# A hybrid decoder layer (HGRN2, S5, two SwiGLU FFNs): interleaved first weight blocks, and a last pair of tiles taken one tile at a time

## What is computed

```
h = concat([meta, x])                                            # 272 x 2048
h = h + 0.5 * swiglu(rms_norm(h, norm_ffn1), gate1, up1, down1)  # width 5632
h = h + mixer(rms_norm(h, norm_mix), ...)                        # HGRN2 + S5 branches, gates, w_out
h = h + 0.5 * swiglu(rms_norm(h, norm_ffn2), gate2, up2, down2)
out = rms_norm(h, norm_final)[16:]                               # 256 x 2048
```

## Time and profile before

| | us |
|---|---|
| median of 3 runs | 2337.34 (2336.91 to 2338.72) |
| the profiled execution | 2339.8 |
| its span, first to last instruction | 2338.1 |
| PE busy | 2308.5 (99%) |
| DVE, ACT, POOL busy | 1522.8, 1025.3, 179.8 |
| DMA, mean over the span | 175 GB/s |

### The profile page before, as it was taken

The page is one execution under the profiler, slowest core; times in us unless marked ns, Lnnn a source line. Parts: engine busy times, 40 slices in busy tenths (PEclk is TensorE's granted clock), DMA queues, the critical chain, the costliest instruction groups (busy, mean ns, idle before and its releaser), DMA issues.

```text
span 2338.1 us, 47313 instructions
## 1 busy us (share of the span) xinstructions
PE 2308.5 (99%) x17952; PEld 2203.8 (94%) x17952; DVE 1522.8 (65%) x2114; ACT 1025.3 (44%) x1251; POOL 179.8 (8%) x250
## 2 busy tenths in 40 slices
PE   8999999999999999999999999999999999999997
PEld 8999999999999999999999999998888888888886
DVE  6555544467554578888877766557776655666655
ACT  5334343445543443334555544445444433444443
POOL 0000010289200000001000000000000000000000
PEclk9999999999999999999999999999999999999999
DMA  7555555555555555554555545655666655656553
GB/s 220 176 174 172 173 175 178 173 172 170 180 174 175 171 166 169 162 170 145 161 158 165 152 143 175 200 186 177 192 181 184 193 187 186 183 183 195 187 187 119
DMA packets 416923, 408.67 MB, mean 175 GB/s; under 512 B 19408, under 2 KB 416720, under 8 KB 416848
## 3 DMA queue, kind: packets, MB, share of 16 engines
q1 hardware_dynamic: 411856, 407.03, 56.4%
q10 hardware_dynamic: 4992, 0.60, 0.2%
HBM read 405.48 MB, written 2.10 MB: 174 GB/s over the span
## 4 chain that ended last, share of the span: by engine, by line
PE 95%; DVE 3%; ACT 1%; issue 1%; DMA 0%; ACTq 0%; DVEq 0%; SPq 0%
PE ps L360 31%; PE ps L358 20%; PE ps L355 20%; PE ps L359 20%; DVE w_lo L899 1%; PE ps L528 0%; ACT w_hi L597 0%; PE ps L472 0%; DMA raw<-gate 0%; PE ps L521 0%; DVE scr L923 0%; DVE ks L1165 0%; ACT xs L619 0%; DVE qs L1166 0%; DVE h L1357 0%
## 5 line engine op out<-in xcount | busy, mean ns | idle before, releaser
L899 DVE TENSOR_TENSOR w_lo<-raw,w_hi 128x1024 fp32r<-128x1024 f32 x765 | 948.5, 1245 | 618.7 <-ACT w_hi L597 612.4
L360 PE MATMUL ps<-xs,w_lo 128*128 128x256 f32 (+2 forms) x4416 | 1258.3, 285 | 0.0
L597 ACT ACTIVATE w_hi<-raw 128x1024 fp32r<-128x1024 f32 x765 | 804.8, 1058 | 967.4 <-PE ps L360 959.9
L358 PE MATMUL ps<-xs,w_hi 128*128 128x272 f32 (+2 forms) x3008 | 864.5, 287 | 6.5 <-DVE w_lo L899 3.6
L359 PE MATMUL ps<-xs,w_hi 128*128 128x272 f32 (+2 forms) x3008 | 861.8, 287 | 0.0
L360 PEld LDWEIGHTS ps<-xs,w_lo 128*128 128x128 f32 x4416 | 833.9, 189 | 0.0
L358 PEld LDWEIGHTS ps<-xs,w_hi 128*128 128x128 f32 x3008 | 567.8, 189 | 11.7 <-issue 8.3
L359 PEld LDWEIGHTS ps<-xs,w_hi 128*128 128x128 f32 x3008 | 570.8, 190 | 0.0
L355 PE MATMUL ps<-xs,w_hi 128*128 128x512 f32 x1408 | 493.3, 395 | 0.3 <-DVE w_lo L899 0.3
L360 PE MATMUL ps<-hs,w_lo 128*128 (+2 forms) x1408 | 402.7, 286 | 0.0
L355 PEld LDWEIGHTS ps<-xs,w_hi 128*128 128x128 f32 x1408 | 264.5, 188 | 61.4 <-issue 0.6
(11 more groups left out here) (250 smaller groups left out, 1587.8 us busy)
## 6 DMA issues: line engine op xcount, KB each, us to landing
raw<-gate SPq DMA_DIRECT2D x176, 512.0 KB, 4.5
raw<-up SPq DMA_DIRECT2D x176, 512.0 KB, 3.8
raw<-down SPq DMA_DIRECT2D x176, 512.0 KB, 3.4
raw<-w_in SPq DMA_DIRECT2D x168, 512.0 KB, 3.5
raw<-w_out SPq DMA_DIRECT2D x32, 512.0 KB, 4.5
raw<-w_proj SPq DMA_DIRECT2D x24, 512.0 KB, 4.5
raw<-glu_a SPq DMA_DIRECT2D x8, 512.0 KB, 3.4
raw<-glu_b SPq DMA_DIRECT2D x8, 512.0 KB, 3.5
```

The costliest lines, as they stand in the source:

```text
L358: pe.matmul(out, hi, xh, start=start and k == 0, stop=False)
L360: last = pe.matmul(out, lo, xh, start=False, stop=stop and k == KT - 1)
L597: act.activation(w_hi[:, slot, :, :], raw[:, slot, :, :], ACT.Copy).then_inc(hi_ready, 1)
L899: tt(w_lo[:, slot, :, :], raw[:, slot, :, :], w_hi[:, slot, :, :].bitcast(f32), SUB).then_inc(lo_ready, 1)
```

## The change

At the start, gate and up units alternate: for each group `g` of four input tiles the gate unit (u = 2g) and the up unit (u = 2g + 1). The first group and its gate unit are loaded, split and multiplied in pieces of one or two tiles, and the next three units are split in halves. Meta tokens and `x` come as one array, so a row of a tile is 272 floats in one piece. The small parameters are loaded by SyncE in the second gate block. The norm stands ahead of unit 6. The warm-up has 9 matmuls of `ones` by `ones`.

At the end, the last pair of tiles is not wide and is taken tile by tile, with squares of its own; the two accumulators of squares are folded to one; the square root's table is loaded a pair earlier; VectorE makes all products, the first two tiles singly.

```diff
+STORES = ((0, 1), (1, 2)) + tuple((k, k + 2) for k in range(2, DT, 2))
-POOL_PAIRS = (3, 7)
@@ SyncE
             def load(j, w, group, col, u):
-                sp.wait_ge(lo_ready, u + 1)
+                if not isinstance(u, int) or u >= RING:
+                    sp.wait_ge(lo_ready, u + 1)
...
+            def load_x(k0, k1, landed):
+                sp.dma_start(h[:, k0:k1, :], hT.rearrange("(k p) t -> p k t", p=P)[:, k0:k1, :]).then_inc(landed, 16)
+            def load_first(w_gate, w_up):
+                for c, (k0, k1) in enumerate(((0, 1), (1, 2), (2, 4))):
+                    load_x(k0, k1, x_first[c] if c < 2 else x_in[0])
+                    sp.dma_start(raw[:, 0, k0:k1, :], w_gate.rearrange("(k p) n -> p k n", p=P)[:, k0:k1, 0:NC])\
+                        .then_inc(w_first[c] if c < 2 else raw_ready[0], 16)
+                for g in range(4):
+                    if g:
+                        load_x(4 * g, 4 * g + 4, x_in[g])
+                        load(2 * g % RING, w_gate, g, 0, 2 * g)
+                    load((2 * g + 1) % RING, w_up, g, 0, 2 * g + 1)
...
-                        column_block(w_gate, 0, 0, load_x)
-                        column_block(w_up, 0, 1)
-                    with sp.Fori(peeled, blocks) as b:
+                        load_first(w_gate, w_up)
+                        column_block(w_gate, NC, 2, load_small)
+                        column_block(w_up, NC, 3)
+                    with sp.Fori(2 * peeled, blocks) as b:
...
+            for c, (k0, k1) in enumerate(STORES):
+                sp.wait_ge(y_final, c + 1)
+                sp.dma_start(out[:, k0:k1, :], h[:, k0:k1, META:T]).then_inc(stored[c % 4], 16)
@@ TensorE
+                    if by_tile and c == 0 and k == KT - 1:
+                        last.then_inc(tile_done, 1)
...
-                        unit(j, (g + q) * 4 + j, 2 * j, n, rhs, start, stop, wide=wide)
+                        unit(j, (g + q) * 4 + j, 2 * j, n, rhs, start, stop,
+                             wide=wide and not (final and j == 3), by_tile=final and stop and j == 3)
...
+                if index == 3:
+                    total = ps[:, NORM_BANK[index], 0:T - c0]
+                    pe.wait_ge(tile_sq, 1)
+                    pe.matmul(total, ones[:, :], scr[:, 2, c0:T], start=True, stop=False)
+                    pe.wait_ge(folded, 1)
+                    pe.matmul(total, ones[:, :], scr[:, 4, c0:T], start=False, stop=False)
+                    pe.wait_ge(sq_ready, 8 * index + 8)
+                    pe.matmul(total, ones[:, :], scr[:, 3, c0:T], start=False, stop=True).then_inc(sq_used, 1)
+                    return
...
+                    def first_blocks():
+                        pe.wait_ge(gated, 1)
+                        pe.wait_ge(hidden, 1)
+                        for u in range(2 * RING):
+                            g, s = u // 2, u % 2
+                            if u == 6:
+                                norm(0, 0)
+                            unit(u % RING, u, 2 * s, T, rows(xs, 4 * g, 0, T), g == 0, g == 3, 4 * g)
...
-            pe.wait_ge(consts, 2)
-            keep_warm(14, 0)
+            pe.wait_ge(ones_ready, 1)
+            keep_warm(9, 0)
+            pe.wait_ge(consts, 1)
@@ ScalarE
+            def last_square(c):
+                if c:
+                    act.wait_ge(pair_out, 4 * PASSES_BEFORE[3])
+                else:
+                    act.wait_ge(summed, 6 * 3 + 5)
+                    act.wait_ge(tile_out, 1)
+                ins = act.activation(scr[:, 2 + c, META:T], h[:, DT - 2 + c, META:T], ACT.Square)
+                ins.then_inc(sq_ready if c else tile_sq, 1)
...
-                            if k == 7:
+                            if k == (6 if f else 7):
                                 load_sqrt()
+                            if f and k == 7:
+                                last_square(1)
+                                return
                             square(1 + 2 * f, c0, k)
+                            if f and k == 6:
+                                last_square(0)
...
+            first_split(1)
+            next_x(1)
+            first_split(2)
+            first_split(3)
+            next_x(2)
+            square(0, 0, 0)
+            square(0, 0, 1)
+            split(0, 1)
+            next_x(3)
+            square(0, 0, 2)
+            split(0, 2)
@@ VectorE, the last pass
+                        def residual_tile(c):
+                            row = h[:, DT - 2 + c, c0:T]
+                            if c == 0:
+                                dve.wait_ge(tile_done, 1)
+                            stt(row, ps[:, 6 + c, 0:T - c0], 0.5, row, MUL, ADD).then_inc(pair_out if c else tile_out, 1)
...
                         def add(j, p=p):
+                            if f and p and j == 3:
+                                residual_tile(0)
                             if 4 * p + j >= 2:
                                 add_squares(1 + 2 * f, c0, 4 * p + j - 1)
+                            if f and p and j == 3:
+                                dve.wait_ge(summed, 6 * 3 + 6)
+                                tt(scr[:, 4, c0:T], scr[:, 4, c0:T], scr[:, 5, c0:T], ADD).then_inc(folded, 1)
...
+            for k0, k1 in STORES:
+                dve.wait_ge(gained, k0 // 2 + 1)
+                y = h[:, k0:k1, META:T]
+                tt(y, y, scr[:, 5:6, META:T].broadcast_to([P, k1 - k0, SEQ]), MUL).then_inc(y_final, 1)
```

More of the change, by code:

```diff
@@ L340, in _, with unit @@
             pe.sem_inc(cx_done, 1)
-            def unit(j, u, banks, n, rhs, start, stop, need=None, wide=False):
-                pe.wait_ge(lo_ready, u + RING + 1)
+            def unit(j, u, banks, n, rhs, start, stop, need=None, wide=False, by_tile=False):
+                first = isinstance(u, int) and u < RING
+                if not first:
+                    pe.wait_ge(lo_ready, u + RING + 1)
                 by_column = [(c, k) for c in range(2) for k in range(KT)]
@@ L365, in keep_warm @@
                 for _ in range(n):
-                    pe.matmul(ps[:, bank, 0:P], ones[:, :], ident[:, :], start=True, stop=True)
+                    pe.matmul(ps[:, bank, 0:P], ones[:, :], ones[:, :], start=True, stop=True)
             def halves_of(x):
@@ L649, in block @@
                     def block(b, mean=False):
-                        for j in range(1 if mean and not f else 0, 4):
-                            split(b * 2 + q, j)
+                        start = mean and not f
+                        if not start:
+                            for j in range(4):
+                                split(b * 2 + q, j)
                         if mean:
                             root(2 * f, c0)
-                        split(b * 2 + q + 1, 0)
+                        split(b * 2 + q + 1, 2 if start else 0)
                         act.wait_ge(gated, b + done + 2)
                         act.activation(scr[:, 2:4, c0:T], scr[:, 0:2, c0:T], ACT.Sigmoid).then_inc(sig_ready, 1)
-                        for j in range(1, 4):
+                        for j in range(3 if start else 1, 4):
                             split(b * 2 + q + 1, j)
@@ new lines, in first_split, with next_x @@
+            def first_split(u):
+                act.wait_ge(raw_ready[u], 16)
+                for half in (slice(0, KT // 2), slice(KT // 2, KT)):
+                    act.activation(w_hi[:, u, half, :], raw[:, u, half, :], ACT.Copy)\
+                        .then_inc(hi_ready if half.start else first_hi, 1)
+            def next_x(g):
+                act.wait_ge(x_in[g], 16)
+                for k in range(4 * g, 4 * g + 4):
+                    upper(0, 0, k)
+            first_split(1)
+            next_x(1)
@@ L745, in _ @@
+            split(1, 0)
+            split(1, 1)
             ffn(0, 0, 0, parameters)
```

187 lines of the change are left out of this document (107 added, 80 removed).

## The result

| | us |
|---|---|
| median after, 7 runs | 2329.56 (2329.07 to 2331.26) |
| median before, beside them, 7 runs | 2337.60 (2336.91 to 2338.72) |
| ratio | 0.9967 [0.9957, 0.9976] |
| the profiled execution after, and its span | 2329.07, 2327.4 |

The change wins 8.0 us, or 7.8 against the median shown ahead. The prediction was 2325.9 with a range up to 2329.3: faster, as forecast, but 3.7 us short of the forecast and 0.3 outside its range.

A forecast was written before the change was run, and what follows sets the result against it. TensorE, busy throughout the middle, bounds the kernel, so only start and end can win: 8.2 + 1.2 + 2.2 - 0.15 = 11.4 us off the 2337.34 median gives 2325.9 us, range 2322.3 to 2329.3.

The forecast's parts named there:

- First piece: Kernel start: small first loads are in SBUF by about 4 us, so TensorE begins near 5.5 instead of 10.83.
- The stream: Start's loads: 5.37 MB up to the last x group, at 0.366 MB/us after 4 us, give its use at 17.8.
- behind it: From last x group to unit 8: splits, squares, norm and units 5 to 7 end at 34.5, 8.2 us won.
- Small loads move ... I take nothing: Seven small loads on SyncE's queue ahead of units 8 to 11: no cost; about 1 us once if cover failed.
- The end: Behind the last matmul: the root starts 1.2 us sooner; products and stores take 8.1 instead of 10.3, 2.2 us won.
- price of the five units: Five units no longer wide make 8 more matmuls each: cost between nothing and 0.5 us, taken as 0.15.
- The median of the runs is 2.5 lower: Conversion from the profiled execution, 2339.8, to the runs' median: a constant 2.5 us lower, so the gain applies in full.
- The first, the handing over slower than its parts: Start: costlier small copies, stream nearer 315 GB/s, a clock fall before the norm; start wins 5 to 6; chance 0.10.
- The second, the clock in the middle moving: Middle, low clock behind the 1351 us hole: the spell vanishes (2322.7) or a second comes (2329.1); chance 0.12.
- The third, the lower clock up to unit 8: Start: broken work keeps the lower clock until unit 8, which begins at 53; 2344 us, slower; chance 0.03.
- The fourth, only the first piece early: Start: last x is late anyway and only the first piece early; start wins 3, 2331 us; chance 0.05.
- What would show it: Signs in the changed profile: times for first matmul, last x, norm, unit 8, root and products, and no 0.50 clock between 10 and 40.

The follow-up runs named there:

- e4: The changed kernel with the first x group and first gate unit as one whole load each: median 2328.75 us, ratio 0.9960 to before.
- e1: The changed start with the end of before: median 2332.70 us, 5.5 us under before, ratio 0.9977.
- e5: The changed kernel repeated unaltered: median 2329.86 us, 8.6 us under before, ratio 0.9964.
- e13: The changed kernel run a third time, unaltered: median 2329.65 us, 8.9 us under before, ratio 0.9960.
- e11: Repeat of the changed kernel with first x group and first gate unit as whole loads: median 2329.23 us, 8.1 us under before, ratio 0.9961.
- e10: Repeat of the changed kernel with first x group and gate unit in two pieces of two tiles: median 2329.35 us, ratio 0.9962 to before.
- e8: Before, with only the seven small loads moved from ScalarE's to SyncE's queue and the three additions behind them: median 2334.99 us, 3.4 us under before.
- e3: Before, with VectorE making all last products and SyncE storing in nine pieces: median 2336.37 us, 1.9 us under before, ratio 0.9993.
- e2: The start of before with the changed end: median 2334.90 us, 3.3 us under before, ratio 0.9987.
- e9: The changed kernel with first x group and gate unit in pieces of one and three tiles: median 2328.83 us, 8.5 us under before, ratio 0.9963.
- e6: The changed kernel with the first gate unit's three pieces issued from ScalarE's queue: median 2329.66 us, 8.8 us under before, ratio 0.9963.
- e7: The changed kernel with first x group and gate unit in two pieces of two tiles, not three: median 2328.38 us, ratio 0.9958 to before.
- e12: Whole loads of first x group and gate unit in the changed kernel, with 16 warm-up matmuls instead of 9: median 2328.47 us, ratio 0.9959 to before.

## Why the prediction was right, and where it was wrong

**What bounds the kernel**: right. The middle has no idle TensorE to win, and the time went where it was sought, ahead of unit 8 and behind the last matmul.

**"First piece", near 5.5**: right (5.14), and nearly worthless by itself: e4 starts 2.8 us later and reaches unit 8 sooner, because the last load sets unit 8.

**"The stream", last x group at 17.8**: this is the step that failed; ScalarE first used it at 20.01. The prediction took the landing as the bytes queued up to that load at the best rate of a stretch of before. With it falls unit 8 at 34.5, since "behind it" was forecast as 16.7 us (34.5 less 17.8) and is 16.72 (36.73 less 20.01), norm and root included. The whole error of the start, 8.2 forecast and 6.0 found, is this one term. It has two parts.
- The rate. 0.45 MB by 4 us was right (4.00 x 0.106 is 0.42). Then 285 GB/s to 6.5 and 352 to 16 us stand where 366 was assumed: 0.20 and 0.13 MB, together about 0.9 us. e4's 369 shows that the first 0.6 of it is the pieces'. The same 2.5 us carry 265, 260 and 253 GB/s in e1, e5 and e13.
- The amount. 5.37 MB are queued up to and with that load, but by its landing 19.98 x 0.295 = 5.89 MB had flowed: about half a MB of the loads queued behind had passed. That is 1.4 us, less the 0.4 allowed for the semaphore. Rate and amount together make 1.9 of the 2.2. In e4 it is much the same, 0.306 x 18.95 = 5.80 MB, but it is no constant: the eleven traces of the new order have 5.72 (e11) to 6.28 MB (e10), so 0.3 to 0.9 passed. That something passes could have been read beforehand, as this stretch of before shows:

```profile
0.00:15.68 15.68, 10.20 (x61) 9.85 (x62) 8.48 (x14) 10.50 (x20) 2.76 (x13) 1.00 0.91 268
```

In before the last x group landed at 15.68, when 4.20 MB had flowed, with 3.74 MB queued up to it (four x loads and three gate units of 0.524 and 0.07 of meta tokens and gain): the same 0.46 MB too many. So loads behind it were well under way by its landing. How much passes was not varied on purpose, so its cause stays open. Nor was the order of SyncE's issues: in after the last x group is issued at 11.88 only, behind units 4 and 5, whose loads wait for VectorE's `w_lo`. The stream ran at 347 to 387 GB/s in each us from 9 to 20 and so was never dry, but whether an earlier issue would bring that load forward was not tried.

**"Small loads move ... I take nothing"**: right as a cost, wrong as a whole, since the gain of the same edit was never priced. By e8 the move is worth 3.4 us of time, and it takes unit 8 from 42.69 (or 41.22, e3) to 38.91; the rest of the new start (interleaving, pieces, meta tokens with x, warm-up) adds 38.91 less 36.73, 2.2 us (in the medians 5.5 of e1 less 3.4). No run takes these four apart, but for the pieces. The sum hid this, since it built the new start from nothing instead of from before's.

**The end**: right. Root 1.28 in the traces for 1.2 forecast, products and stores 1.9 for 2.2; e2's time 3.3 for 3.4. The nine products last 4.97 us for 5.0 forecast; the missing 0.3 is in the stores' data, which begin at 294 and 290 GB/s where 353 was taken throughout:

```profile
2320.30:2321.00 0.70, 0.00 (x0) 0.00 (x0) 0.70 (x3) 0.00 (x0) 0.00 (x0) 0.79 0.87 294
2321.00:2322.00 1.00, 0.00 (x0) 0.00 (x0) 1.00 (x2) 0.00 (x0) 0.00 (x0) 0.50 0.87 290
```

The **price of the five units** no longer wide (0.15) isn't seen: the middle takes 2277.6 in after and 2277.9 in e1, which keeps them wide, both at a clock of 0.50 for some 3.4 us.

**"The median of the runs is 2.5 lower"**: the second step that failed. The sum was made against one execution and then shifted by a constant. But before's profiled execution held a stretch at 0.50 at the start and the longer one in the middle, which other executions of the same start (e3) or of one and the same program (after, e5, e13) have only in part. What the change took from that execution it couldn't take in full from the median. Of the 3.6 us between 11.4 and 7.8 the stream is 2.2, the end 0.1, and 1.3 is left for this. In the profiled executions the gain is 10.7 for 11.4 forecast; in the medians it is 7.8 to 8.9. Built against e3's unit 8, the same parts give 41.22 less 36.73, 4.5, and 3.2 of the end: 7.7, at the low end of the medians'. e1's 5.5 lies between this 4.5 and the 6.0 of the profiled executions, at the edge of its theory A. Before's 67 timed executions fall roughly into three groups, 24 from 2336.5 to 2337.7, 29 from 2337.9 to 2338.8 and 14 from 2339.2 to 2340.3; the profiled one, 2339.8, is of the slowest. The groups' means are some 1.4 us apart, about the price of one spell, but the timed executions have no trace, so that the spells make them is argued and not shown.

**Rivals.** The first, the handing over slower than its parts with a stream nearer 315 GB/s, came nearest, with a start of 5 to 6 us; at 2328.1 to 2329.1 it fell 0.5 short of the measured time. Its slower stream is near half of what happened. The small copies did not cost more than estimated (0.40 to 0.42 us for 256), no hole ahead of the norm let the clock fall, and the bytes that pass the last x group are not in it. The second, the clock in the middle moving, happens between executions of one program; whether the change has a part in it is not shown. The third, the lower clock up to unit 8, did not come: in after the records drop to 0.29 us at 6.8 and stay there, with holes of 1.12, 0.89, 0.69 and 0.50. (The granted clock of 1.00 is no proof of it, since e11 has 1.00 over its 27 slow matmuls.) The Trainium skill's rule of bursts with waits for DMA ("TensorE: Matmul & The Clock Gate", section "HAM oscillation — how this bites in real kernels") is borne out in the new order by e9 alone, once, behind 1.76 us, and there it cost nothing. The fourth, only the first piece early, is refuted by unit 8's 6.0.

**"What would show it"**: first matmul, clock, root, products and tail came as written (5.14; no 0.50 between 10 and 40; 2.07 behind the last matmul's end; none above 0.69; 8.4, near the 8). Last x, norm (28.75 for 26 to 27) and unit 8 (36.73 for 34 to 35.5) did not, all three by the same 2.2 us or less.

## What to carry to other kernels

Where a queue of loads sets the start, find the last load that the critical work needs and read from the old trace how many bytes had flowed when such a load landed, not how many were queued ahead of it, and allow a range, since here it moved by 0.6 MB between programs and by 0.3 between executions of one; an early first piece can be worth nothing. Look at what an engine does with its own queue: moving ScalarE's small loads, two of them scattered, gave more here (3.4 us by the medians) than all the rest of the new start (2.1). And before a gain is taken from one profiled execution to the median, see whether it holds stretches of lower clock that other executions of the same program don't have.

## What the runs showed of the hardware that was not expected

- Small first loads went with a slower stream from 4 to 6.5 us: 253 to 285 GB/s with three pieces a tensor on one queue (after, e1, e5, e13), 307 on two queues (e6), 283 and 314 with two pieces (e7, e10), 328 with one and three tiles (e9), 369 and 370 with whole loads (e4, e12 and e11). A faster stream there did not always mean an earlier last x group (e6, e10).
- 0.3 to 0.9 MB of later loads flowed before the last x group's landing (0.46 in before, 0.5 in after, 0.4 in e4, 0.9 in e10), and between executions of one program the landing varied by 0.2 to 0.75 us at the same rate.
- ScalarE stood still while its queue issued scattered DMAs: 2.97 us for two of 128 KB. SyncE took 3.11 and 5.82 us over the same two.
- A hole in TensorE's work was followed by a lower clock or not with no clear difference in its length: 2.13 and 2.75 us yes and 2.21 no (before, e2, e3), 1.76 yes and 1.79 no (e9, e10).
- With 2.28 us between warm-up and first real matmul 27 matmuls ran as at the lower level (0.43 us a record, e11), though the granted clock reads 1.00; with a warm-up up to the first real matmul the records were at 0.29 from the second on (e12).
- VectorE's 512-wide products took up to 1.75 us while GpSimd made its own, and 0.68 alone (e1, e3).
